# Two output gate tiles of the mLSTM as one seven-product unit ahead of the sliding attention, and the filler beside it in every second unit

## The reference, cut to what matters

```python
h = rmsnorm(x, norm_mix_g[i])
proj = h @ w_in[i]
qk_ml, v_ml, o_ml, if_pre, q_sw, k_sw, v_sw, g_a, g_b = jnp.split(proj, split_idx, axis=-1)
...
h_ml = mlstm_chunkwise(q_ml, k_ml, v_ml.reshape(B, S, ML_HEADS, ML_DV), ig, lf)
...
y_a = jax.nn.sigmoid(o_ml) * h_ml
y_b = swa_with_sinks(q_sw, k_sw, v_sw, sinks[i])     # 16 heads of 64, window 128
merged = jax.nn.sigmoid(g_a) * (y_a @ w_branch_a[i]) + jax.nn.sigmoid(g_b) * (y_b @ w_branch_b[i])
```

## Time and profile before

| | us |
|---|---|
| three runs, median | 2712.03 (2711.83 to 2712.18) |
| the profiled execution | 2712.3 |
| its span | 2710.5 |
| granted PE clock over the span, of full speed | 0.997 |
| PE busy | 2678.6 (99%) |
| PEld, DVE, POOL, ACT busy | 2052.8, 1318.8, 844.9, 513.8 |

### The profile page before, as it was taken

How to read it: one execution, slowest core, us unless ns; L and a number is a source line. 1 busy time by engine, 2 the same in 40 slices (tenths; PEclk the granted TensorE clock), 3 DMA queues, 4 the chain that set the end, 5 groups by cost and what they waited for, 6 DMA issues and landing times.

```text
span 2710.5 us, 31061 instructions
## 1 busy us (share of the span) xinstructions
PE 2678.6 (99%) x12346; PEld 2052.8 (76%) x12346; DVE 1318.8 (49%) x2582; ACT 513.8 (19%) x1179; POOL 844.9 (31%) x698
## 2 busy tenths in 40 slices
PE   8999999999999999999999999999999999999998
PEld 3655555556886478888888888985578888888887
DVE  7657555567227564334332345327463325544433
ACT  3100000004117361122000102116420011000012
POOL 0434343342313004402443432420044404444420
PEclk9999999999999999999999999999999999999999
DMA  6334333323220102222222221220012222222220
GB/s 260 128 113 137 108 113 115 98 78 137 94 55 19 55 1 78 86 78 81 91 94 78 93 94 63 82 91 18 32 63 93 78 78 93 92 79 93 80 100 32
DMA packets 58464, 233.85 MB, mean 86 GB/s; under 512 B 4944, under 2 KB 17104, under 8 KB 45008
## 3 DMA queue, kind: packets, MB, share of 16 engines
q1 hardware_dynamic: 47648, 196.17, 21.0%
q0 software_dynamic: 8352, 31.46, 3.5%
q10 hardware_dynamic: 2320, 4.24, 0.5%
HBM read 227.66 MB, written 2.10 MB: 85 GB/s over the span
## 4 chain that ended last, share of the span: by engine, by line
PE 61%; DVE 1%; ACT 0%; issue 0%; DVEq 0%; ACTq 0%
PE banks L799 42%; PE banks L714 11%; PE banks L792 2%; PE banks L850 1%; PE banks L1484 1%; PE banks L1421 1%; PE banks L1403 1%; PE banks L961 0%; PE banks L1486 0%; PE banks L1478 0%; PE banks L1359 0%; PE banks L1492 0%; PE banks L1462 0%; PE banks L765 0%; PE banks L766 0%; PE banks L1339 0%
## 5 line engine op out<-in xcount | busy, mean ns | idle before, releaser
L3169 POOL TENSOR_TENSOR big<-weight_ring 128x512 f32<-128x512 f32 (+2 forms) x125 | 151.7, 1214 | 1265.9 <-PE banks L799 671.4
L799 PE MATMUL banks<-big 128*128 128x256 f32 (+1 forms) x2096 | 533.7, 402 | 0.0
L799 PEld LDWEIGHTS banks<-big 128*128 128x128 f32 x2096 | 397.6, 190 | 104.0 <-DVE rpb_rows L2378 2.5
L799 PE MATMUL banks<-big,weight_ring 128*128 128x256 f32 (+1 forms) x1384 | 363.8, 407 | 0.0
L799 PE MATMUL banks<-normed,weight_ring 128*128 128x256 f32 (+1 forms) x1328 | 346.3, 404 | 1.7 <-issue 0.9
L799 PEld LDWEIGHTS banks<-big,weight_ring 128*128 128x128 f32 x1384 | 262.8, 190 | 75.2 <-DVE scratch_b L2384 0.7
L799 PEld LDWEIGHTS banks<-normed,weight_ring 128*128 128x128 f32 x1328 | 252.1, 190 | 69.1 <-issue 1.7
L3170 POOL TENSOR_TENSOR big<-weight_ring 128x512 f32<-128x512 f32 (+2 forms) x150 | 223.8, 1492 | 0.0
L714 PE MATMUL banks<-normed,weight_ring 128*128 128x256 f32 (+2 forms) x816 | 219.4, 424 | 3.6 <-ACT normed L1643 3.2
L799 PE MATMUL banks<-normed,big 128*128 128x256 f32 (+1 forms) x896 | 216.4, 389 | 0.0
L799 PEld LDWEIGHTS banks<-normed,big 128*128 128x128 f32 x896 | 170.2, 190 | 31.7
(11 more groups left out here) (497 smaller groups left out, 3505.9 us busy)
## 6 DMA issues: line engine op xcount, KB each, us to landing
weight_ring<-weights SPq DMA_DIRECT2D x144, 1024.0 KB, 4.8
rpb_rows<-w_ada POOLq DMA_DIRECT2D x28, 512.0 KB, 3.6
p_embed<-w_ada POOLq DMA_DIRECT2D x28, 512.0 KB, 3.6
weight_ring<-weights SPq DMA_DIRECT2D x16, 768.0 KB, 4.3
weight_ring<-weights SPq DMA_DIRECT2D x15, 512.0 KB, 3.6
big<-w_ada SPq DMA_DIRECT2D x2, 1536.0 KB, 11.0
residual<-xT SPq DMA_DIRECT2D x3, 1024.0 KB, 15.3
big<-w_ada SPq DMA_DIRECT2D x3, 1024.0 KB, 17.0
```

The lines of the kernel that those rows point to most:

```text
L799: last = nc.tensor.matmul(z, stationary(p), moving(p), start=opens and p == 0, stop=p == kp - 1, skip_group_check=True)
L3169: T(w[2], a11, a21, ALU.subtract).then_inc(sums_c, 1)
```

## The change

Tiles 0 and 1 of the output gate become a unit of their own, o_ma, with the number V_OG at the end of V_MIX: made by seven products between V_QSW[3] and if_m, into the rows PE2 (the buffer p_embed). The other three units of the weights stream as o_mb behind if_m. Beside the attention only tiles 2 and 3 are made, 16 steps in place of 32, one in each unit of odd number. All counts of the semaphores og["done"] and og["act"] are lower by two. PE's wait ahead of the attention is for V_OG in place of V_QSW[3]. ACT waits in `output_gates` for V_OG's parts. The places of the eight tiles change: 0 and 1 in PE2, 2 to 7 in the first six rows of rpb_rows. The number of every later unit goes up by one.

```diff
--- before.py
+++ after.py
@@ -66,7 +66,8 @@
     ("up2c", "up2", 8, 3, UNIT), ("up2d", "up2", 19, 3, UNIT),
     ("down2b", "down2", (1, 0, 8), 4, UNIT), ("down2c", "down2", (None, 8, 3), 4, 12 * P),
     ("qk_m", "qk_m", 0, 4, UNIT), ("k_sw", "k_sw", 0, 1, UNIT), ("v_sw", "v_sw", 0, 1, UNIT),
-    ("v_m", "v_m", 0, 4, UNIT), ("q_sw", "q_sw", 0, 4, UNIT), ("if_m", "if_m", 0, 1, KC * 36), ("o_m", "o_m", 0, 4, UNIT),
+    ("v_m", "v_m", 0, 4, UNIT), ("q_sw", "q_sw", 0, 4, UNIT), ("o_ma", "o_m", 0, 1, UNIT),
+    ("if_m", "if_m", 0, 1, KC * 36), ("o_mb", "o_m", 1, 3, UNIT),
     *((f"merge2_{o}{q}{at // 8}", "merge2", (q, at, 8, o), 1, UNIT) for o in range(4) for q in (1, 0) for at in (0, 8)),
     ("out2", "out2", 0, 4, UNIT), ("embed", "ple", (None, KC, 2, 1), 1, KC * P),
     ("up3a", "up3", 0, 8, UNIT), ("down3a", "down3", (0, 0, 8), 4, UNIT), ("up3b", "up3", 8, 4, UNIT),
@@ -141,7 +142,8 @@
 ROWS_BY_K = (V_VSW, *V_VM)
 TOKENS_OUT = (*ROWS_BY_K, V_PROJ[4], V_PROJ[5])
 V_QSW = [_fast(SEQ["q_sw"] + m, 4, True) for m in range(4)]
-V_MIX = [*V_QK, V_KSW, V_VSW, *V_VM, *V_QSW]
+V_OG = _fast(SEQ["o_ma"], 4, True)
+V_MIX = [*V_QK, V_KSW, V_VSW, *V_VM, *V_QSW, V_OG]
 V_BEFORE2 = len(FAST)
 V_MERGE2 = _merges("merge2", (1, 0), 8)
 V_FFN3 = len(FAST)
@@ -236,7 +238,7 @@
 
 
 
-OG_BANK = (7, 7, 7, 7, 4, 5, 7, 7)
+OG_BANK = (None, None, 7, 7, 4, 5, 7, 7)
 OG_IN_GATES = (4, 5)
 OG_AFTER = ((6, range(0, 4)), (6, range(4, 8)), (7, range(0, 4)), (7, range(4, 8)))
 
@@ -440,7 +442,7 @@
         MR2 = view(big, 0, KC, S)
         LATE_GATES = view(big, 0, 4, KC * P)
 
-        OG = [view(bias_t, 0, 6, S)[:, b, :] if b < 6 else PE2[:, b - 6, :] for b in range(8)]
+        OG = [PE2[:, b, :] if b < 2 else view(bias_t, 0, 6, S)[:, b - 2, :] for b in range(8)]
 
         ROWS = view(big, 12288, 6, S)
         ACOL = big[:, 19456:19456 + 16].rearrange("p (c h) -> p c h", c=4)
@@ -587,6 +589,8 @@
 
             if v in V_QK:
                 return QK, 4 + 2 * V_QK.index(v)
+            if v == V_OG:
+                return PE2, 0
             return (KS_RAW, 0) if v == V_KSW else (QS, 2 * V_QSW.index(v))
 
         def value_rows(u, m, l):
@@ -1391,8 +1395,8 @@
                     last = mm(bank[64 * e:64 * e + 36, 6, :], slot(n, (k + e) * 36, 36), H[:, k + e, 0:S], k == 0,
                               k == KC - 2, k + e == 0)
             last.then_inc(gate["pre"], 1)
-            pe.wait_ge(c11, copied_upto(V_QSW[3]))
-            pe.wait_ge(took, 5 * (V_QSW[3] + 1))
+            pe.wait_ge(c11, copied_upto(V_OG))
+            pe.wait_ge(took, 5 * (V_OG + 1))
             pe.wait_ge(prj2["scaled"], 2)
 
 
@@ -1426,12 +1430,12 @@
                 return last
 
             def og_step(b, k):
-                n = SEQ["o_m"] + b // 2
+                n = SEQ["o_mb"] + b // 2 - 1
                 if k == 0:
                     if b % 2 == 0:
                         begin(n)
-                    if b not in (0, *OG_IN_GATES):
-                        pe.wait_ge(og["act"], b)
+                    if b not in (2, *OG_IN_GATES):
+                        pe.wait_ge(og["act"], b - 2)
                 last = mm(bank[:, OG_BANK[b], :], slot(n, ((b % 2) * KC + k) * P, P), H[:, k, 0:S], k == 0,
                           k == KC - 1, b % 2 == 0 and k == 0)
                 if k == KC - 1:
@@ -1442,10 +1446,8 @@
                     og_step(b, k)
 
             def og_beside(i):
-                if i % KC:
-                    og_step(i // KC, i % KC - 1)
-                if i % KC == KC - 1:
-                    og_step(i // KC, KC - 1)
+                if i % 2:
+                    og_step(2 + i // (2 * KC), i % (2 * KC) // 2)
 
             attention(asw, 32, sw_scores, sw_pieces, transposed, sw_values, asw["max"], (4, 5), 1, 4, 1, og_beside)
 
@@ -1492,7 +1494,7 @@
                     last = nc.tensor.matmul(bank[:, 1, :], ones, NUM_SQ[:, v, :], start=(v == 0), stop=(v == 1))
                 last.then_inc(ml["ssq"], 1)
 
-            pe.wait_ge(og["act"], 4)
+            pe.wait_ge(og["act"], 2)
             og_steps(4, range(KC))
             og_steps(5, range(0, 4))
             gate_columns()
@@ -1503,7 +1505,7 @@
             ml_score(0, 1)
             for h in range(X_HEADS):
                 if h == 0:
-                    pe.wait_ge(og["act"], 6)
+                    pe.wait_ge(og["act"], 4)
                 else:
                     pe.wait_ge(ml["num"], 2 * h)
                     pe.wait_ge(ml["acc"], h)
@@ -2094,12 +2096,12 @@
                 A(stat_col(u, 6, 2), stat_col(u, 4, 2), ACT.Exp).then_inc(asw["biased"], 1)
 
             def og_rows(b):
-                act.wait_ge(og["done"], b + 1)
+                act.wait_ge(og["done"], b - 1)
                 A(OG[b], bank[:, OG_BANK[b], :], ACT.Copy).then_inc(og["act"], 1)
 
             def og_beside(i):
-                if i and i % KC == 0:
-                    og_rows(i // KC - 1)
+                if i and i % (2 * KC) == 0:
+                    og_rows(1 + i // (2 * KC))
 
             attention(asw, 32, sw_exp, lambda u: [256 if u % 4 == 0 else 512],
                       lambda u, q, w: TMP5[:, u % 2, 0:w], (4, 5), lambda u: u - 1, False, og_beside)
@@ -2154,8 +2156,11 @@
                 if h % 2:
                     og_rows(OG_AFTER[h][0])
             def output_gates():
+                act.wait_ge(took, 5 * (V_OG + 1))
+                act.wait_ge(c11, copied_upto(V_OG))
                 for b in range(8):
-                    act.wait_ge(og["act"], b + 1)
+                    if b >= 2:
+                        act.wait_ge(og["act"], b - 1)
                     A(OG[b], OG[b], ACT.Sigmoid).then_inc(og["gate"], 1)
             for o in range(4):
                 for q in (1, 0):
```

## The result

The changed kernel takes 2720.49 us (median of 8 runs, 2719.96 to 2721.9), the kernel before 2712.14 in the same comparison (8 runs, 2711.74 to 2713.42): a ratio of 1.003, 95% interval 1.0021 to 1.004. It is 8.35 us slower; I had said 7.5 us more than 2712.03, that is 2719.5.

What follows compares the result with a forecast made beforehand. PE was taken as the bound (99% busy), with DVE not far behind in the attention. 12.09 us added, 14.1 removed from PE, 9.6 back as waits: +7.5 on 2712.03, so 2719.5 us, range 2714.8 to 2723.5.

Steps and rivals of the forecast that it cites:

- The three bounds that it names: Error margins: 1.4 us for 0.2 in each group's wait, 0.6 for the opening, 0.5 for the parity.
- The unit, 12.09: Ahead of the attention: one more seven-product unit adds 12.09 us to the path, PE busy throughout.
- the parity: Every later unit's parity flips, moving its zones and weight sums to the other half: costed at nothing, within 0.5 us.
- The wait for DVE, 0.89 a group: Before unit 6's transposes, once a group: DVE needs 4.71 us after the scores, PE's work 3.82; PE waits 0.89.
- the dearer transposes: In 16 attention units transposes stand straight behind scores: 0.05 us more each, 0.8 in all, counted against PE's removed work.
- The wait for ACT, 0.23: After unit 6's transposes, once a group: PE waits another 0.23 us for ACT's copy before unit 5's values.
- The opening: Attention's start: filler behind units 2 and 4 covers little; 1.0 and 0.4 us of its saving come back.
- one more slow stretch: One more half-clock stretch in the attention's opening, +1.6 us, said to lie within the main case.
- B: Rival: no waits come in the attention, all 14.1 is gained, -2.0 us, 2710.0; chance 5%.
- D: Rival: in the new unit POOL's four sums are late and stand bare, +4.8 us, 2724.3; chance 4%.
- B2: Rival: the pair's copy slips out of DVE's run; 4.2 us less comes back, +3.3, 2715.3; chance 11%.
- C: Rival: each attention group's waits drop the clock to half, 11.2 us on top, 2730.7; chance 6%.

Runs made afterwards that it cites:

- e2: Changed kernel with the same 16 filler steps in units 4k+2 and 4k+3 instead of 4k+1 and 4k+3: 2714.57 us.
- e3: Changed kernel with DVE's copy of a finished pair of heads cut from 512 to 16 columns: 2716.90 us.
- e4: Changed kernel without the new unit, so tiles 0 and 1 of the output gate are never made: 2708.36 us.
- e1: Kernel before with the new unit added ahead of the attention and all 32 filler steps kept: 2724.94 us.
- e8: e2 with its filler steps cut from 512 to 16 tokens, leaving out most of tiles 2 and 3: 2714.54 us.
- e9: Kernel before, its 32 filler steps placed at waits or slack (8 in units 1 to 4, five in the last two units): 2707.69 us.
- e7: Changed kernel with its 16 steps re-placed: 8 in units 1 to 7, 8 ahead of the later groups' waits: 2712.26 us.
- e5: Changed kernel with three unread 128x512 matmuls added in the attention's opening, where PE waits for DVE: 2718.53 us.
- e6: Kernel before with the same 32 filler steps, two each in units 2 and 3, none doubled in units 7 and 15: 2709.91 us.

## Why the prediction was right

It held in its direction, in its mechanism and within a microsecond in its sum, the last in part by luck: two terms that were off by 1.6 and 0.6 us had opposite signs. (The three bounds that it names, 1.4, 0.6 and 0.5, add up to 2.5 us and not to the 2.2 of its "2717.3 to 2721.7"; nothing hangs on it.) By its steps:

- **The unit, 12.09.** Measured 12.09 in three kernels. That the parity and the later stages cost nothing held: 801.6 us behind the attention in both kernels.
- **The wait for DVE, 0.89 a group.** Measured 0.76. DVE's end of it was exact, 4.71. PE's end was 3.95 instead of 3.82: 0.05 of this are the dearer transposes, which I had put into another term, and 0.08 are the scores of unit 8: I had counted 0.42 for them, from one row's start to the next, but where PE waits behind them nothing overlaps their end, and they take their whole record, 0.49 (1856.68). e2 and e3 show the mechanism from both ends: a step ahead of the wait removes it, half a microsecond off DVE's run takes as much off it.
- **The wait for ACT, 0.23.** Measured 0.20. The group came out at 9.42 for 9.5.
- **The opening.** The transposes of unit 2 were to come 0.53 earlier: 1846.23 - 1835.82 = 10.41 after the first scores, before 1834.68 - 1823.74 = 10.94. But then the clock stayed at half for a second stretch, and by unit 6's scores the changed kernel was 1.1 behind the one before (1852.60 - 1835.82 = 16.78 against 1839.41 - 1823.74 = 15.67). With the 0.53 it should have been 0.5 ahead, so the opening is 1.6 worse than the sum has it. This is the term that was mis-sized: the prediction named one more slow stretch at 1.6 us, but kept it out of the sum; the clock loss went from 1.7 to 3.4. With it 7.5 becomes 9.1, less 0.6 for seven groups of 9.42 and not 9.5 it is 8.5, for 8.3 measured. The stage by the window of the earlier trace rows is 81.99 for some 81.2.
- **Rivals.** B (PE the bound) and D (the unit dearer) fell with the trace after, with e4 and e1. B2 fell with e3. C, the clock falling in every group, did not come: the group's window has 1.00, and in e8 PE was busy only 45.62 of 54.27 us, with waits in each group, at 1.00. The rule of the Trainium skill ("TensorE: Matmul & The Clock Gate", section "A second HAM failure mode: psum-queue depth-cycling") that often repeated short idles make the clock swing does not show in these float32 matmuls at idles of 0.47 and 0.66 us (e8) or 0.76 us (the changed kernel) once in each group of 8.5 to 9.4 us; the section's own case is a bf16 kernel.

## What to carry to other kernels

Filler work is worth what it covers, and that depends on the place: draw the second engine's run from one product to the moment PE needs its result, add up PE's own work over the same stretch, and put the filler where that sum is the smaller one. Before making the filler cheaper, find out how long the stage would be with none: here 16 steps of 0.86 us at the right places cost nothing (the groups of e2 and e8), and 16 more on top of them cost 8.0 us of attention (e9 against e7), so 12.09 us of faster products ahead of the stage were the dearer way to make the same two tiles. The same work in another order is a cheap test, as it leaves PE's work as it was; of the other terms it can still move the clock.

## What the runs showed of the hardware

Added work in an idle stretch made the kernel faster by 2.0 us (e5), since the granted clock did not fall behind it. That fall is not a function of PE's idle time alone. In e1's profiled execution PE waits in the opening as long as in the earlier trace rows:

```profile
1842.63 0.66 PE L964 MATMUL banks<-consts_sb,scratch_a 128*128 128x128 f32 x4 [1.35 <-DVE scratch_a L3019]
1844.15 0.44 PE L1424 MATMUL banks<-scratch_b,big 128*64 128x128 f32 x4 [0.86 <-DVE big L3008]
```

that is 1.35 and 0.86 us against 1.36 and 0.86, and yet the clock stays at 1.00 through the window of 1835.70 shown above. In the kernel before the same idle time was followed by 1.7 us of loss, in the changed one, with 0.89 more, by 3.4, in e8, with the most idle time, by 5.1. What decides it in a single execution I did not find out; with the stage filled (e5, e6, e7, e9) the profiled executions lost nothing. e1's five runs lie in two clumps, 2723.71 and 2723.86, and 2724.94 to 2725.51; the traced one is in the lower. That the upper ones lost the 1.7 us which this one did not is argued, not shown, as only one execution has a trace. The granted clock over the span, which every run has, points the same way: of the kernel before's 73 runs beside the experiments the eight fastest, 2710.94 to 2711.16, all have 0.998, and the twelve slowest, 2713.22 to 2713.97, all have 0.996. So part of a kernel's spread, and some 1 to 2 us between two medians, can be the clock's; a difference of a few us is to be read from the stage's rows as well.
